# First queries and r times k made ahead of the second memory logits, chunk products of four heads beside the memory attention, sums over heads in one bank

## What is computed

```
r, k, v, d_lo, a_lo, g_lo = jnp.split(p_tm, RWKV_SPLITS, axis=-1)
kk = l2_normalize(heads(k * a_k_k, RWKV_HEADS))
k = k * (1.0 + (lr - 1.0) * a_k_a)
y = rwkv7_scan(rh, heads(decay, RWKV_HEADS), kh, vh, -kk, kk * lrh)
y = head_group_norm(y, a_lnx_g, a_lnx_b)
y = y + jnp.sum(rh * kh * a_r_k, axis=-1, keepdims=True) * vh
m = memory_attention(heads(q_mem, MEM_HEADS), mem_n, a_mem_kv)
x = x + jnp.concatenate([y_mix, m], axis=-1) @ a_w_out
```

## Time and profile before

| | us |
|---|---|
| median of 3 runs | 1143.61 (1142.79 to 1145.05) |
| profiled execution, its own time | 1146.87 |
| its span in the profile | 1145.6 |
| PE busy | 1115.3 (97%) |
| DVE busy | 732.5 (64%) |
| ACT busy | 569.6 (50%) |

### The profile page before, as it was taken

The page is one execution under the profiler, slowest core; times in us unless marked ns, Lnnn a source line. Parts: engine busy times, 40 slices in busy tenths (PEclk is TensorE's granted clock), DMA queues, the critical chain, the costliest instruction groups (busy, mean ns, idle before and its releaser), DMA issues.

```text
span 1145.6 us, 22502 instructions
## 1 busy us (share of the span) xinstructions
PE 1115.3 (97%) x9837; PEld 1062.9 (93%) x9837; DVE 732.5 (64%) x1042; ACT 569.6 (50%) x771; POOL 65.5 (6%) x130
## 2 busy tenths in 40 slices
PE   8999999999999999999799999999999999999998
PEld 8898899889999999988688999999987899999998
DVE  5557776455655555668988856555578875655553
ACT  6355655354544444674344544444466764443343
POOL 2400112000000000100000000000002000000000
PEclk9999999999999999999899999999999999999999
DMA  7944455335455554533000545555554224555551
GB/s 264 314 146 145 150 184 184 134 107 185 178 186 186 189 188 164 208 118 141 2 3 3 179 172 189 188 186 189 187 197 184 74 104 175 186 187 189 188 187 39
DMA packets 29862, 182.70 MB, mean 159 GB/s; under 512 B 3591, under 2 KB 6872, under 8 KB 8900
## 3 DMA queue, kind: packets, MB, share of 16 engines
q1 hardware_dynamic: 24608, 174.07, 42.3%
q0 software_dynamic: 1888, 4.75, 1.5%
q10 hardware_dynamic: 3268, 2.43, 0.7%
HBM read 180.18 MB, written 1.07 MB: 158 GB/s over the span
## 4 chain that ended last, share of the span: by engine, by line
PE 85%; DVE 7%; ACT 4%; issue 2%; DMA 1%; POOL 1%; ACTq 0%; DVEq 0%; POOLq 0%
PE bank L683 81%; DVE w_lo L1505 2%; ACT w_hi L2334 1%; DMA w_raw<-in_weights 1%; PE bank L697 1%; PE bank L880 1%; PE bank L687 0%; DVE inverse L2224 0%; DVE inverse_t L2249 0%; DVE chunk_products L2204 0%; PE bank L1227 0%; PE bank L1246 0%; ACTq L2523 0%; ACT squares_n L2617 0%; DVE x_channels_lo L1603 0%
## 5 line engine op out<-in xcount | busy, mean ns | idle before, releaser
L1505 DVE TENSOR_TENSOR w_lo<-w_raw,w_hi 128x2048 fp32r<-128x2048 f32 x157 | 358.2, 2291 | 192.0 <-ACT w_hi L2334 191.6
L2334 ACT ACTIVATE w_hi<-w_raw 128x2048 fp32r<-128x2048 f32 x161 | 306.5, 1914 | 111.6 <-DMA w_raw<-in_weights 106.7
L683 PE MATMUL bank<-x_channels_hi,w_hi 128*128 128x256 f32 x1424 | 230.3, 285 | 2.0 <-DVE memory_queries L2080 0.9
L683 PE MATMUL bank<-x_channels_lo,w_hi 128*128 128x256 f32 x1424 | 227.9, 283 | 0.0
L683 PE MATMUL bank<-x_channels_hi,w_lo 128*128 128x256 f32 x1424 | 220.8, 278 | 0.0
L683 PEld LDWEIGHTS bank<-x_channels_hi,w_hi 128*128 128x128 f32 x1424 | 195.5, 191 | 5.5 <-issue 3.8
L683 PEld LDWEIGHTS bank<-x_channels_lo,w_hi 128*128 128x128 f32 x1424 | 193.9, 190 | 0.1
L683 PEld LDWEIGHTS bank<-x_channels_hi,w_lo 128*128 128x128 f32 x1424 | 191.6, 189 | 0.0
L683 PE MATMUL bank<-hidden_hi,w_hi 128*128 128x256 f32 x528 | 102.1, 281 | 1.3 <-ACT hidden_hi L2611 1.3
L683 PE MATMUL bank<-hidden_hi,w_lo 128*128 128x256 f32 x528 | 103.3, 284 | 0.0
L683 PE MATMUL bank<-hidden_lo,w_hi 128*128 128x256 f32 x528 | 101.8, 280 | 0.0
(11 more groups left out here) (451 smaller groups left out, 1543.6 us busy)
## 6 DMA issues: line engine op xcount, KB each, us to landing
w_raw<-in_weights SPq DMA_DIRECT2D x163, 1024.0 KB, 4.8
mem_rows<-in_mem POOLq DMA_DIRECT2D x2, 1024.0 KB, 6.4
xn<-in_x SPq DMA_DIRECT2D x1, 1024.0 KB, 5.3
w_raw<-in_weights SPq DMA_DIRECT2D x2, 512.0 KB, 8.4
bias<-bias_rows ACTq DMA_DIRECT2D x2, 512.0 KB, 9.1
bias<-bias_rows ACTq DMA_DIRECT2D x1, 1024.0 KB, 10.9
out<-xn SPq DMA_DIRECT2D x4, 256.0 KB, 2.2
wide_masks<-in_triangle_masks POOLq DMA_DIRECT2D x1, 832.0 KB, 8.4
```

The lines of the kernel that those rows point to most:

```text
L683: return nc.tensor.matmul(out, lhs, rhs, start=start, stop=stop)
L1505: V.tensor_tensor(k.w_lo[:, s, :], k.w_raw[:, s, :], k.w_hi[:, s, :].bitcast(F32), ALU.subtract).then_inc(k.lo_done, 1)
L2334: A.activation(k.w_hi[:, s, :], k.w_raw[:, s, :], ACT.Copy).then_inc(k.hi_done, 1)
```

## The change

- DVE makes the first half of the queries and r times k in turn 1 of m0 and the second half of the queries in turn 2; the raw pairs of `ain5` come in turn 3; masks of heads 0 and 1 in turn 4. `r_k` becomes three tiles at places of their own.
- PE makes the sums over heads of the first two blocks in turn 2, the chunk products of heads 0 and 1 in turn 3, those of heads 2 and 3 and the second sums in turn 4. The third sums come behind the products of heads 6 and 7. All sums go to bank 0, one after the other, and ACT empties it between. The chunk products go round banks 4, 5, 1, 2, 6, 7.
- DVE waits for all sums before the first inverse.

```diff
-        self.fac, self.rk = work("key_factor", 30, [P, RWB, S]), in_channels("r_k", 6.125, [P, RWB, S])
+        self.fac, self.rk = work("key_factor", 30, [P, RWB, S]), [work(f"r_k_{n}", kb, [P, 2, S]) for n, kb in enumerate((80, 87, 21.5))]
+RK_BANK, PRODUCT_BANK = 0, (4, 5, 1, 2, 6, 7)
```

On PE:

```diff
-    attention("m0", beside_m0)
-    PE.wait_ge(*k.exped.all("m0"))
-    PE.wait_ge(*k.pt.all("m0"))
-
-    for h in range(0, RW_HEADS, 2):
+        if i == 2:
+            PE.wait_ge(*k.dve_once.at("rk", 0))
+            sums_of_heads(0)
+        if i == 3:
+            PE.wait_ge(*k.exped.all("m0"))
+            chunk_products(0)
+        if i == 4:
+            PE.wait_ge(*k.raw_made.all("ain"))
+            chunk_products(2)
+            sums_of_heads(1)
+
+    def sums_of_heads(n):
+
+        if n:
+            PE.wait_ge(*k.act_once.at("rk", n - 1))
+        matmul(bank[RK_BANK][:, :].rearrange("p (k t) -> p k t", k=2), k.same_head[:, :], k.rk[n][:, :, :], True,
+               True).then_inc(k.pe_once.sem, 1)
+
+    def chunk_products(h):
+
         if h in (0, 6):
             PE.wait_ge(*k.dve_once.at("r", h // 6))
-        if h == 10:
-            PE.wait_ge(*k.dve_once.at("rk", 0))
-            PE.wait_ge(*k.raw_made.all("ain"))
-            for n in range(3):
-                matmul(bank[n][:, :].rearrange("p (k t) -> p k t", k=2), k.same_head[:, :], k.rk[:, 2 * n:2 * n + 2, :], True,
-                       True).then_inc(k.pe_once.sem, 1)
-        if h >= 4:
-            PE.wait_ge(*k.g_v.at("heads", h - 3))
+        if h >= 6:
+            PE.wait_ge(*k.g_v.at("heads", h - 5))
         for c in range(NC):
             for q in range(2):
                 r0 = 64 * q
-                m = matmul(bank[4 + (h + q) % 4][:, c * P:(c + 1) * P], bk[r0:r0 + 64, h // 2, c, :], ar[r0:r0 + 64, h // 2, c, :], c == 0,
-                           c == NC - 1)
+                m = matmul(bank[PRODUCT_BANK[(h + q) % 6]][:, c * P:(c + 1) * P], bk[r0:r0 + 64, h // 2, c, :],
+                           ar[r0:r0 + 64, h // 2, c, :], c == 0, c == NC - 1)
                 if c == NC - 1:
                     m.then_inc(k.g_p.sem, 1)
+    attention("m0", beside_m0)
+    PE.wait_ge(*k.pt.all("m0"))
+    chunk_products(4)
+    chunk_products(6)
+    sums_of_heads(2)
+    chunk_products(8)
+    chunk_products(10)
```

On DVE:

```diff
-        if i in (2, 3):
-            if i == 2:
-                V.wait_ge(*k.shifted.at("sh", SHIFTED.index(5)))
-                V.wait_ge(*k.dve.so_far())
-            V.tensor_tensor(queries(i - 2), of_chunks(rB, i - 2), decays(k.down, i - 2, 1), ALU.mult).then_inc(k.dve_once.sem, 1)
-        if i == 4:
-            raw_pair(5, 0)
-            raw_pair(5, 1)
+            V.wait_ge(*k.shifted.at("sh", SHIFTED.index(5)))
+            V.wait_ge(*k.dve.so_far())
+        if i in (1, 2):
+            V.tensor_tensor(queries(i - 1), of_chunks(rB, i - 1), decays(k.down, i - 1, 1), ALU.mult).then_inc(k.dve_once.sem, 1)
+        if i == 1:
             for b in range(RWB):
...
             r.then_inc(k.dve_once.sem, 1)
+        if i == 3:
+            raw_pair(5, 0)
+            raw_pair(5, 1)
+        if i == 4:
+            masked(0)
+            masked(1)
+
+    def masked(h):
+        V.wait_ge(*k.g_p.at("heads", h))
+        V.tensor_tensor(k.g[h][:, :, :], bank[PRODUCT_BANK[h % 6]][:, :].rearrange("p (c z) -> p c z", c=NC),
+                        k.masks[:, 0:2, :].rearrange("p a t -> p (a t)").unsqueeze(1).to_broadcast((P, NC, 2 * C)),
+                        ALU.mult).then_inc(k.g_v.sem, 1)
...
-        for h in range(6 * half, 6 * half + 6):
+        for h in range(6 * half + (0 if half else 2), 6 * half + 6):
             masked(h)
+        if half == 0:
+            V.wait_ge(*k.pe_once.all("rk"))
         first_inverse(half)
```

On ACT:

```diff
+    def sums_kept(n):
+        A.wait_ge(*k.pe_once.at("rk", n))
+        A.activation(k.rest[:, 2 * n:2 * n + 2, :], bank[RK_BANK][:, :].rearrange("p (t s) -> p t s", t=2),
+                     ACT.Copy).then_inc(k.act_once.sem, 1)
+
     def beside_m0(i):
+        if i == 3:
+            sums_kept(0)
         if i >= 4:
             keep_pair(5, i - 4)
     attention("m0", beside_m0)
     split["end"] = k.total_units
-    for n in range(3):
-        A.wait_ge(*k.pe_once.at("rk", n))
-        A.activation(k.rest[:, 2 * n:2 * n + 2, :], bank[n][:, :].rearrange("p (t s) -> p t s", t=2), ACT.Copy).then_inc(k.act_once.sem, 1)
+    sums_kept(1)
+    sums_kept(2)
```

More of the change, by code:

```diff
@@ L2181, in beside_m0 @@
                             k.up[:, :, 1:NC, 0:1].rearrange("p b c o -> p b (c o)"), ALU.mult).then_inc(k.dve_once.sem, 1)
-        if i in (2, 3):
-            if i == 2:
-                V.wait_ge(*k.shifted.at("sh", SHIFTED.index(5)))
-                V.wait_ge(*k.dve.so_far())
-            V.tensor_tensor(queries(i - 2), of_chunks(rB, i - 2), decays(k.down, i - 2, 1), ALU.mult).then_inc(k.dve_once.sem, 1)
-        if i == 4:
-            raw_pair(5, 0)
-            raw_pair(5, 1)
+            V.wait_ge(*k.shifted.at("sh", SHIFTED.index(5)))
[3 more added lines that the diff above has]
+        if i == 1:
             for b in range(RWB):
-                r = V.scalar_tensor_tensor(out=k.rk[:, b, :], in0=rB[:, b, :], scalar=k.col("a_r_k_2", b), in1=kB[:, b, :], op0=ALU.mult,
-                                           op1=ALU.mult)
+                r = V.scalar_tensor_tensor(out=k.rk[b // 2][:, b % 2, :], in0=rB[:, b, :], scalar=k.col("a_r_k_2", b), in1=kB[:, b, :],
+                                           op0=ALU.mult, op1=ALU.mult)
                 if b < RWB - 1:
@@ L2200, in side_columns @@
         return k.masks[:, n:n + 1, :].to_broadcast((P, 6, C))
[L2202 to L2206, removed]
     def first_inverse(n):
```

## The result

The changed kernel took 1147.12 us (median of 18 executions, 1143.96 to 1150.64) against 1144.31 us of the kernel before on the same chip (1142.79 to 1146.76, also 18). The ratio is 1.0022, 95% interval 1.0014 to 1.003: by the ratio some 2.5 us slower (the medians differ by 2.8), where I had forecast 0.8 and a range up to 1146.8. The range was laid around 1143.61 for the kernel before; its median beside the changed kernel was 0.7 us higher, which is part of why the time lies above the range. Two more sets of 12 executions, on other occasions, gave 1.0012 (1.0 to 1.0024) and 1.0015 (1.0004 to 1.0027). The centre of the excess is nearer to 2 us than to 3, but it is real, and the executions reach further up than those of before: 1150.6 against 1146.8, and over all sets on record 1150.6 against 1148.4.

What follows compares the result with a forecast made beforehand. DVE was taken to set the pace in the changed stretch, though PE is busy 97% overall. Inverse +1.1 and mask wait -0.36 summed to +0.75 us, clock 0: 1144.4 us from the 1143.61 median, range 1142.0 to 1146.8.

Steps and rivals of the forecast that it cites:

- DVE's gap takes r times k and the queries: DVE ahead of head 2's maxima in m0: 3.42 us of work fill a 3.0 us gap; maxima 0.4 us late.
- PE's wait for the sums ends with queries 1: PE ahead of the first sums in m0: semaphore count makes it wait from 539.9 to 542.05 us.
- Values 3 late, DVE idle ahead of output 3, +1.1 at the first inverse, -0.36 at mask 10: DVE's masks and first inverse: 1.2 us idle, inverse +1.1 us, later mask wait gone -0.36; sum +0.75 us.
- The clock: "I take 0": PE's half clock near the start of the recurrence: begins earlier while PE idles, taken as 0; possible -0.7 to +2.7 us.
- the late gap: PE's idle ahead of chain 1's first step: 5.3 us instead of 3.05, low clock at least as sure, counted 0.
- Rival B: Half clock behind PE's new 2.1 us wait in m0: +2.2 to +3.7 us, about 1146.6 us; chance 0.13.
- The low clock in the first levels: Recurrence's first steps on PE at 1.2 GHz: expected to cover the same work as before, counted 0.
- the case that I had priced at -0.7: Low clock at the recurrence's start ends earlier, so the 48 "first" matmuls are no longer slow: -0.7 us.
- A: Sums in m0 wait for r_k alone, so PE has no wait: -1.2 us, 1142.4 us; chance 0.14.
- C: DVE's stretch closes up with its idle filled and no new idle: -3.4 us, 1140.2 us; chance 0.07.
- D: Nothing counts, as PE is bound later anyway: 1143.6 us; chance 0.08.
- What a measurement can tell: Whole kernel's time: a measurement tells 0.2% (2.3 us) from nothing, not less; no measurable change forecast.

Runs made afterwards that it cites:

- e1_count: Changed kernel with the semaphore's events declared in the order they happen, so the sums wait for r_k alone: 1143.88 us, ratio to before 0.9984.
- e2_after_warm: Changed kernel plus 40 idle transposes on PE in its late gap, before the wait for chain 1's first turn: 1146.41 us, ratio to before 1.0013.
- e7_rk_alone: Kernel before with only first queries and r times k moved into DVE's gap, semaphore in order, r_k in two tiles: 1144.23 us, ratio 0.9998.
- e3_before_warm: Kernel before plus 24 idle transposes on PE in its late gap of 3.05 us: 1143.34 us, ratio 0.9992.
- e9_reordered_warm: Changed kernel, semaphore in order, r_k in two tiles, masks 0-3 in turn 4, sums later, 42 transposes in late gap: 1142.26 us, ratio to before 0.9976.

## Why the prediction was wrong

All executions with a clock on record, counted over the sets (mean clock 0.992 or less; mean time; 1148.5 us or more, which is just above the highest of before, 1148.4):

| kernel | executions | low clock | mean us | high |
|---|---|---|---|---|
| before | 103 | 4 | 1144.93 | 0 |
| changed | 42 | 17 | 1146.86 | 9 |
| changed, wait filled | 24 | 6 | 1144.97 | 0 |
| before, with the wait | 12 | 10 | 1147.45 | 2 |

- **DVE's gap takes r times k and the queries; head 2's maxima 0.4 us late, output 0 as before.** Right: they are 3.43 and 4.67 us behind `state_factor` (537.59 and 538.83 less 534.16), before 3.24 and 4.67; the delay is 0.2.
- **PE's wait for the sums ends with queries 1.** Right, 2.11 us, and shown by `e1_count`, where it vanishes once the declaration follows the order of the events (and the waits on the second half of the queries with it).
- **Values 3 late, DVE idle ahead of output 3, +1.1 at the first inverse, -0.36 at mask 10.** Right in kind and nearly in size: 1.50 us of idle for 1.2, 0.36 us at the wait for the sums for 0 to 0.1, so the first turn comes 1.33 us later; behind it 0.46 us are won for 0.36. Together +0.87 for +0.75.
- **The clock: "I take 0".** This is the step that failed. In the sum I weighed only the late gap and put nothing for the new wait of 2.1 us, with 0.13 for rival B, because PE had idled 1.81 us ahead of 549.15 and kept its clock. One trace of one execution cannot bear that: of three traces of the changed kernel two keep full clock behind the wait, and the third is at 1.2 GHz from 540.6 to 547.4 us. Rival B's place and price are borne out by that trace (a 7 us stretch for 2.86 us; I had 2.9 for one of the same length). It should have been part of the forecast as a share of executions. By the table, filling the wait takes 1146.86 - 1144.97 = 1.9 us off the mean, and that is nearly the whole excess over before (1.93). At 2.9 to 3.2 us for one stretch that would be, as an estimate, some six in ten executions; no run counts them, as the mean clock does not single them out.
- **Why the order's +0.87 is not visible beside it.** The low clock in the first levels, also put at 0, came out at -0.55 to -0.72: from the second turn to `y_rest` the three traces of the changed kernel take 12.87, 12.70 and 12.71 us for 13.42 before. Two of them, with the attention at full clock, are thus +0.32 and +0.14 us up to `y_rest`, and those of the filled wait +0.18 and -0.15. That agrees with the filled kernel's mean, 0.04 us over before. It rests on one trace of the kernel before; the same kernel with the wait alone took 12.72 us there.
- **The late gap.** Right that it starts the low clock earlier against the second turn (3.1 us ahead of it in the first trace, 1.5 us behind it in the kernel before) and costs nothing more. Its end came earlier too, the case that I had priced at -0.7. Filling it gained nothing in `e2_after_warm`, where the low clock came later and fell on PE's steps.
- **Rivals.** A is the kernel `e1_count`: its stretch to the second turn is 0.72 + 0.46 = 1.18 us shorter than before, as forecast (-1.2), and its ratio of 0.9984 is -1.8 us with an interval that holds it. C did not come, for the reason given: DVE waits 1.50 us for values 3. D was not so, as the time moved with the wait.
- **What a measurement can tell.** I had set 0.2% as the least that can be told from nothing; with 18 executions the interval was 0.08% to either side, so the slowdown is clear of noise.

What stays open: what decides in which execution the clock falls, and in how many it falls in the attention, why `e7_rk_alone` gained nothing in time, and the 0.3 us of mask 4.

## What to carry to other kernels

When work is moved so that a nearly full TensorE gets a new idle of 2 to 3 us amid small matmuls, count a chance of half clock behind it, and price it by matmuls of the same shape at either level; then look at the spread over many executions and at more than one profile, as one may show the lucky case and the mean clock does not say where the clock was down. The direct test is to fill the idle and leave the order as it is. When instructions that count up one semaphore are reordered, the stages' declaration must be reordered too, or waiters wait for the last of them. And here an engine's queue order (an output ahead of masks on DVE, sums ahead of values on PE) decided more than how much work was moved into a gap: 3.4 us of DVE work were moved, and the second turn came 0.87 us later.

## What the runs showed of the hardware that was not expected

An idle of 2.75 us on TensorE stood right ahead of some 7 us at 1.2 GHz (540.6 to 547.4) in one execution; idles of 2.11 and 2.10 us in two other executions of the same kernel with the same order did not bring it. The Trainium skill (TensorE: Matmul & The Clock Gate, Part 1) warns of idle gaps longer than this one; by that rule alone this wait would have passed as safe, and the measured times say otherwise. Filling an idle with transposes left no low clock at PE's next steps in two kernels (`e3_before_warm`, `e9_reordered_warm`); in a third one (`e2_after_warm`) the clock fell 7.2 us behind the second turn instead, amid the steps.
